# Reordering VectorE's work at the head of the feed-forward stages, and the last two weight loads of each

## The chip, the cores and the metric

The kernel runs on one core of a Trainium2 chip. The metric is device time in microseconds (us) for one execution. The kernel before the change took 2425.06 us (median of 3 runs, 2421.0 to 2426.04). The engines are named as the profile names them: PE is TensorE's matmul, PEld its weight load, DVE VectorE, ACT ScalarE, POOL GpSimd, SP SyncE, which here only issues the loads of the weights.

## What is computed

Two transformer layers work on 256 tokens of width 1024. Each layer has a feed-forward stage, a mixing stage (attention and a convolution) and a second feed-forward stage. After them comes a third, different block, which the change does not touch. All of it is in 32-bit floating point.

```
for l in range(2):
    x = x + 0.5 * swiglu(rms_norm(x, ffn1_norm[l]), gate[l], up[l], down[l])    # F = 2816
    ... attention and convolution on rms_norm(x, mix_norm[l]) ...
    x = x + 0.5 * swiglu(rms_norm(x, ffn2_norm[l]), gate2[l], up2[l], down2[l])
    x = rms_norm(x, post_norm[l])
swiglu(x) = (silu(x @ w_gate) * (x @ w_up)) @ w_down
ada = silu(c) @ w_ada + b      # 48 column tiles; used only by the later block
```

## The kernel before

**Panels.** Weights come from memory in panels of 128 x 1024 numbers (512 KB). SP loads them, in one fixed order, into a ring of 7 slots (`ring`); each load has a wait of its own, for the work that frees its slot, and SP passes its waits in order. A feed-forward stage takes 66 weight panels: for each of its 22 tiles of hidden width a gate panel, an up panel and a down panel. The numbers of its panels are 0 gate, 1 up, 2 gate, 3 up, 4 down, then in each round of a loop with 10 rounds 5, 6 (gate, up), 7 (down), 8, 9 (gate, up), 10 (down), and at the end 65 (down).

**Two halves of a panel.** A product is made of three matmuls on operands that are split into a high and a low part. ACT writes the high part of a panel into one of three slots of `wsplit` (`high`, L1372) as soon as the panel has landed and the panel three before it has been used; DVE writes the low part (`low`, L1998) after that. PE waits for the low part (`low_ready`). A gate or up panel is 24 matmuls of L716, a down panel 12 of L756.

**The hidden activations.** When the up panel of a tile is through, ACT computes the silu (L1467) and DVE multiplies and splits (`gated`, three instructions, L2072 to L2076, which end in `act_ready`). The down panel of the tile waits for that.

**The ada shares.** Of the 48 panels of `w_ada`, 12 are put into each of the four feed-forward stages and worked off by DVE beside the matmuls: one panel is a share, 16 instructions (`ada_products`, L2046 x2 and L2050 x14) that add up in `ada_acc`; PE then adds over partitions (`ada_sum`, L769). Share 0 is loaded ahead of panel 4; share 11 is loaded at the end, its products (`ada_last`) are computed in the stage that follows, and `ada_out` (L2063) puts the 24 sums of a stage into `ada`. In PE's order `ada_sum` of share 0 stands between panel 4 and panel 5, and waits for the products.

**The order.** Every engine's order is that of the code, written out by hand. DVE's at the head of a stage is: low part of panel 3, `gated(0)`, low part of panel 4, half of share 0, low part of panel 5, the rest of share 0, and the loop. In layer 1's first feed-forward stage the products of share 11 of the stage before stand in pieces among the preparations (`spare` in `row_factors`, where DVE waits for ACT) and around panel 3. `normed` (L2033, two instructions) scales the rows of the residual; it stands at the end of the first feed-forward stage of each layer. At the end of a stage SP issues the load of panel 65 (waiting for the low part of panel 59), then that of share 11 (waiting for the products of share 10); the first load of the next stage waits for the low part of panel 65.

In what follows the four feed-forward stages are called F1 (it begins at 16 us), F2 (365), F3 (569) and F4 (911).

## Time and profile before

| | |
|---|---|
| time, median of 3 | 2425.06 us |
| profiled execution: time, span | 2425.06 us, 2423.4 us |
| mean granted TensorE clock | 0.969 of full |
| PE busy | 2285.3 us (94%) |
| DVE busy | 1700.5 us (70%) |
| ACT busy | 1108.0 us (46%) |
| chain that ended last | PE 37%, DVE 12%, issue 2%, ACT 2% |
| weight panels | 539 loads of 512 KB, 4.2 us to landing (median) |

The span is cut in the profile into stretches, and the busy time of an engine is the sum of its instructions there. A busy engine is not the bound wherever it is busy; the argument goes by what each engine waits for at a given place. The four feed-forward stages take 194 to 201 us each.

### The profile page before, as it was taken

How to read it: one execution, taken by the hardware profiler on the slowest of the kernel's cores; microseconds unless marked ns; L12 is line 12 of the kernel's file. 1: busy time of each engine (PE TensorE's matmuls, PEld its weight loads, DVE VectorE, ACT ScalarE, POOL GpSimd, SP SyncE). 2: the span in 40 equal slices, each digit the busy share in tenths (PEclk: the TensorE clock that was granted, in tenths of full speed). 3: DMA queues.
4: the chain of work that ended last, by engine and by line, in shares of the span. 5: the costliest groups of instructions: out<-in, count | busy, mean ns of one | idle time of the engine just before them, and what ended most of it. 6: DMA issues, size and time to landing. Idle time of an engine off the chain costs nothing.

```text
span 2423.4 us, 37828 instructions
## 1 busy us (share of the span) xinstructions
PE 2285.3 (94%) x13712; PEld 1986.6 (82%) x13712; DVE 1700.5 (70%) x3271; ACT 1108.0 (46%) x1769; POOL 87.3 (4%) x140
## 2 busy tenths in 40 slices
PE   7999989998999989996999999999999999999979
PEld 6998769998998769995777778888887888888868
DVE  6877858778877958786445545443547888888884
ACT  4333344335333244334545553333435655556652
POOL 0000000000000000001112101001100000000000
PEclk9999989999999989997999999999999999999989
DMA  7564216554554216553344432221212222222213
GB/s 272 194 227 163 87 58 253 204 203 182 209 212 178 81 58 235 199 208 72 79 76 78 70 97 69 70 70 62 79 44 102 82 83 81 87 87 87 84 47 104
DMA packets 81766, 298.64 MB, mean 123 GB/s; under 512 B 10132, under 2 KB 10644, under 8 KB 80916
## 3 DMA queue, kind: packets, MB, share of 16 engines
q1 hardware_dynamic: 77904, 284.72, 33.6%
q0 software_dynamic: 2048, 4.20, 3.2%
q10 hardware_dynamic: 1736, 8.67, 1.0%
q8 instruction: 49, 0.80, 0.1%
q14 instruction: 29, 0.24, 0.0%
HBM read 296.51 MB, written 1.05 MB: 123 GB/s over the span
## 4 chain that ended last, share of the span: by engine, by line
PE 37%; DVE 12%; issue 2%; ACT 2%; DVEq 0%; ACTq 0%
PE ps L716 28%; PE ps L1308 2%; DVE work L2709 2%; DVE work L2698 2%; DVE wsplit L1998 2%; PE ps L1166 1%; PE ps L1048 1%; PE ps L1062 1%; PE ps L1038 1%; DVE work L2748 1%; DVE work L2679 1%; DVE work L2677 1%; PE ps L1018 1%; PE ps L1286 1%; DVE work L2682 0%
## 5 line engine op out<-in xcount | busy, mean ns | idle before, releaser
L716 PE MATMUL ps<-hsplit,wsplit 128*128 128x256 f32 (+1 forms) x8328 | 1382.6, 324 | 32.8 <-DVE work L2719 17.7
L716 PEld LDWEIGHTS ps<-hsplit,wsplit 128*128 128x128 f32 x8328 | 1204.1, 192 | 163.4 <-issue 33.4
L1372 ACT ACTIVATE wsplit<-ring 128x1024 fp32r<-128x1024 f32 x465 | 491.1, 1057 | 593.5 <-PE ps L716 458.3
L1998 DVE TENSOR_TENSOR wsplit<-ring,wsplit 128x1024 fp32r<-128x1024 f32 x465 | 571.8, 1231 | 264.6 <-ACT wsplit L1372 262.2
L756 PE MATMUL ps<-wsplit,fsplit 128*128 128x512 f32 x1056 | 256.3, 391 | 0.0
L756 PEld LDWEIGHTS ps<-wsplit,fsplit 128*128 128x128 f32 x1056 | 192.7, 188 | 36.3
L2050 DVE SCALAR_TENSOR_TENSOR work<-ring,cs,work 128x128 f32<-128x128 f32 x672 | 206.1, 348 | 8.8
L1467 ACT ACTIVATE work<-ps 128x256 f32<-128x256 f32 x88 | 33.8, 384 | 159.4 <-PE ps L716 159.4
L2162 DVE SCALAR_TENSOR_TENSOR work<-work,vec 128x256 f32<-128x256 f32 x240 | 100.9, 481 | 1.7
L716 PEld LDWEIGHTS ps<-wsplit,hsplit 128*128 128x128 f32 x768 | 95.5, 197 | 4.5 <-issue 3.0
L716 PE MATMUL ps<-wsplit,hsplit 128*128 128x256 f32 x768 | 97.1, 289 | 1.1 <-DVE wsplit L1998 1.1
L2072 DVE TENSOR_TENSOR work<-ps,work 128x256 f32<-128x256 f32 x88 | 37.3, 424 | 81.2 <-ACT work L1467 81.0
L819 PE MATMUL ps<-work,ring 128*128 128x256 f32 x416 | 91.0, 380 | 0.0
L819 PEld LDWEIGHTS ps<-work,ring 128*128 128x128 f32 x416 | 79.1, 191 | 10.6
L2806 POOL DMA_DIRECT2D work<-rpb x64 | 39.4, 624 | 1273.5 <-DVE xT L2033 1130.4
L1715 ACT ACTIVATE work<-ps 128x512 f32<-128x512 f32 (+1 forms) x64 | 31.4, 491 | 115.5 <-PE ps L1048 114.6
L2410 DVE TENSOR_REDUCE work<-ps 128x2 f32<-128x1024 f32 (+1 forms) x32 | 30.7, 958 | 56.7 <-PE ps L1038 56.2
L1308 PE MATMUL ps<-work 128*128 128x128 f32 x512 | 64.6, 282 | 0.0
L1308 PEld LDWEIGHTS ps<-work 128*128 128x128 f32 x512 | 63.3, 199 | 1.2
L1486 ACT ACTIVATE work<-work 128x512 f32<-128x512 f32 (+2 forms) x42 | 28.9, 687 | 67.7 <-DVE work L2145 50.2
L742 PE MATMUL ps<-cst,work 128*128 128x128 f32 x112 | 22.8, 377 | 34.4 <-DVE work L2016 33.8
L2748 DVE COPY_PREDICATED work<-cst,ps 128x256 f32<-128x256 int32 x112 | 50.2, 448 | 3.9
(331 smaller groups left out, 2305.2 us busy)
## 6 DMA issues: line engine op xcount, KB each, us to landing
ring<-panels SPq DMA_DIRECT2D x539, 512.0 KB, 4.2
work<-latent_weights ACTq DMA_DIRECT2D x2, 2304.0 KB, 13.1
work<-rpb POOLq DMA_DIRECT2D x64, 64.0 KB, 7.1
cst<-constants ACTq DMA_DIRECT2D x1, 1408.0 KB
work<-x SPq DMA_DIRECT2D x1, 1024.0 KB, 5.6
work<-post_rows ACTq DMA_DIRECT2D x2, 512.0 KB, 5.7
cT<-ctx ACTq DMA_DIRECT2D x1, 1024.0 KB, 9.3
out<-xT SPq DMA_DIRECT2D x1, 1024.0 KB, 3.9
```

Of the source, the lines that this page charges most:

```text
L716: ins = mm(out_, w(a), x(b), start=start and n == 0, stop=stop and n == 2, **kw)
L756: ins = mm(ps[:, 2 * t + half, :], lhs(a, t), w[:, b, half * 512:(half + 1) * 512], start=first and a == 0 and b == 0, stop=last and a == 1)
L819: last = mm(ps[:, bank, half * T:(half + 1) * T], w[:, k, :], hf[:, k, :], start=k == 0, stop=k == KD - 1)
L1308: last = mm(ps[:, 4 + r % 2, e * T + s * 128:e * T + (s + 1) * 128], k_, q_, start=True, stop=True)
L1372: af(wsplit[:, split_slot(name, n), 0, :], ring[:, p % slots, :], ACT.Copy).then_inc(high_ready, 1)
L1998: tt(parts[:, 1, :], ring[:, p % slots, :], parts[:, 0, :].bitcast(fp32), ALU.subtract)\
L2050: ins = stt(ada_acc[:, v, :], w[:, k, :], factor, ada_acc[:, v, :], ALU.mult, ALU.add)
L2162: ins = stt(acc[:, c, :], u_pad[:, c, j:j + T], w, acc[:, c, :], ALU.mult, ALU.add)
L2698: ins = tt(c_aq[:, lev, :].rearrange("p (n a g) -> p n a g", n=nb, a=2), own, border, ALU.subtract)
L2709: ins = tt(c_ak[:, lev, :].rearrange("p (n a g) -> p n a g", n=nb, a=2), border, own, ALU.subtract)
L2748: ins = nc.vector.copy_predicated(diag, m.unsqueeze(1).to_broadcast([128, 2, 128]), got)
L2806: pool.dma_start(dst.rearrange("p (a w) -> p a w", a=4), src).then_inc(a_bias_loaded, 16)
```

## The change

DVE, at the head of every feed-forward stage: the low part of panel 4 is no longer computed ahead of the products of share 0, nor that of panel 5 in their middle. All 16 products come first, then the loop begins, and its rounds begin with the low parts of the two panels with which they ended before. PE's order is changed in F3 alone, where `ada_sum` of the stage before moves from between panels 2 and 3 to behind panel 3. In the preparations of F3 the products of share 11 no longer fill DVE's waits: the first 8 stand behind the low part of panel 2, the last 8 behind that of panel 3, and `ada_out` ahead of `gated(0)`. `normed` moves from the end of F1 and F3 to their head. SP issues the load of share 11 ahead of that of panel 65.

```diff
--- before.py
+++ after.py
@@ -673,8 +673,8 @@
                     with sp.Fori(0, FT // 2 - 2) as i:
                         for p in (14, 15, 16, 13, 17, 18, 19):
                             again(p, i)
+                    again(len(s.order) - 2)
                     again(len(s.order) - 1)
-                    again(len(s.order) - 2)
                 elif s.panels % s.slots:
                     for p in range(s.slots, s.panels):
                         again(p)
@@ -784,10 +784,9 @@
                                (rows_done, l * 12 + 8 * f + 4) if last else None, i, ready=(act_ready, ready))
 
                 gate_up(0, 0, wait=lambda k: pe.wait_ge(h_ready, h_at(n) + (k + 1)))
-                project(name, l, 2, ps[:, 5, 0:T])
+                gate_up(2, 1)
                 if l > 0 and f == 0:
                     ada_sum(l - 1, 1, ADA_PER_FFN - 1)
-                project(name, l, 3, ps[:, 5, T:2 * T])
                 down(4, 0, fb + 1, first=True)
                 pe.wait_ge(ada_ready, 2 * l + f)
                 ada_sum(l, f, 0)
@@ -2001,23 +2000,19 @@
             def halves(a, b):
                 return a[:, b // 2, (b % 2) * 512:(b % 2 + 1) * 512]
 
-            def row_factors(q, sq0, per, sets, src, firsts=(), spare=None):
+            def row_factors(q, sq0, per, sets, src, firsts=()):
 
                 for t in range(2):
                     dve.wait_ge(sq_ready, sq0 + per * (t + 1))
                     tt(n_ms[:, t, 0:sets], n_ss[:, t, 0:sets, 0], n_ss[:, t, 0:sets, 1], ALU.add).then_inc(row_stage, 1)
                     if t == 0 and firsts:
                         low(*firsts[0])
-                if spare is not None:
-                    spare(range(0, 2))
                 dve.wait_ge(rstd_ready, 3 * q + 1)
                 for half in range(2):
                     c = slice(half * 512, (half + 1) * 512)
                     ts(xs[:, 0, c], src[:, 0, c], n_rr[:, 0:1], None, ALU.mult).then_inc(row_stage, 1)
                 for first in firsts[1:]:
                     low(*first)
-                if spare is not None:
-                    spare(range(2, 4))
 
             def turned(q, gain, banks, name, l):
 
@@ -2076,20 +2071,16 @@
                     tt(fsplit[:, par, 1, :], ff_sil[:, par, :], fsplit[:, par, 0, :].bitcast(fp32), ALU.subtract)\
                         .then_inc(act_ready, 1)
 
-                if l > 0 and f == 0:
-                    ada_last(l - 1, 1, range(4, 6))
                 low(name, l, 3)
                 if l > 0 and f == 0:
-                    ada_last(l - 1, 1, range(6, KD))
+                    ada_last(l - 1, 1, range(4, KD))
+                    ada_out(l - 1, 1)
                 gated(0, fb + 1)
-                low(name, l, 4)
-                if l > 0 and f == 0:
-                    ada_out(l - 1, 1)
-                ada_products(name, l, f, 4, 0, 0, range(0, 4))
-                low(name, l, 5)
-                ada_products(name, l, f, 4, 0, 0, range(4, KD))
+                ada_products(name, l, f, 4, 0)
                 V.restart()
                 with dve.Fori(0, FT // 2 - 1) as i:
+                    low(name, l, 4, i)
+                    low(name, l, 5, i)
                     gated(1, i * 2 + fb + 2)
                     low(name, l, 6, i)
                     ada_products(name, l, f, 6, 1, i, range(0, 2))
@@ -2099,13 +2090,11 @@
                     gated(0, i * 2 + fb + 3)
                     low(name, l, 9, i)
                     ada_products(name, l, f, 6, 1, i, range(5, KD))
-                    low(name, l, 10, i)
-                    low(name, l, 11, i)
                     V.restart()
+                low(name, l, 3 * FT - 2)
+                low(name, l, 3 * FT - 1)
                 gated(1, fb + FT)
                 V.restart()
-                if f == 0:
-                    normed(l)
                 if f == 1:
                     dve.wait_ge(rows_loaded, l * 32 + 48)
                 dve.wait_ge(x_normed, 2 * (l + 1))
@@ -2313,6 +2302,9 @@
                     dve.wait_ge(ada_sig, 1)
                     V.did(tt(cs[:, 1, :], cs[:, 0, :], vec2[:, W_C:W_C + 16], ALU.mult))
                     V.restart()
+                else:
+                    ada_last(l - 1, 1, range(0, 4))
+                normed(l)
                 ffn("ffn1", l, 0)
                 V.restart()
                 row_factors(l * 3 + 1, 16 * l + 4, 2, 1, xN)
@@ -2323,8 +2315,7 @@
                 ffn("ffn2", l, 1)
                 V.restart()
                 row_factors(l * 3 + 3, 16 * l + 12, 4, 2, xg,
-                            (("ffn1", l + 1, 0), ("ffn1", l + 1, 1)) if l + 1 < LAYERS else (),
-                            (lambda tiles: ada_last(l, 1, tiles)) if l + 1 < LAYERS else None)
+                            (("ffn1", l + 1, 0), ("ffn1", l + 1, 1)) if l + 1 < LAYERS else ())
                 if l + 1 < LAYERS:
                     dve.wait_ge(const_loaded, l * 16 + 112)
             def modulation(j):
```

DVE at the head of F1, as its program has it before: the low parts (L1998) of panels 3, 4 and 5 stand around `gated(0)` and the two halves of share 0.

```order
L1998 TENSOR_TENSOR wsplit<-ring,wsplit 128x1024
L2072 TENSOR_TENSOR work<-ps,work 128x256
L2074 CAST fsplit<-work 128x256
L2076 TENSOR_TENSOR fsplit<-work,fsplit 128x256
L1998 TENSOR_TENSOR wsplit<-ring,wsplit 128x1024
L2046 TENSOR_SCALAR work<-ring,cs 128x128 x2
L2050 SCALAR_TENSOR_TENSOR work<-ring,cs,work 128x128 x6
L1998 TENSOR_TENSOR wsplit<-ring,wsplit 128x1024
L2050 SCALAR_TENSOR_TENSOR work<-ring,cs,work 128x128 x8
```

DVE at the same place now (L1997 is the low part, L2028 is `normed`, L2041 and L2045 the products):

```order
L2028 TENSOR_SCALAR xT<-work 128x1024 x2
L1997 TENSOR_TENSOR wsplit<-ring,wsplit 128x1024
L2067 TENSOR_TENSOR work<-ps,work 128x256
L2069 CAST fsplit<-work 128x256
L2071 TENSOR_TENSOR fsplit<-work,fsplit 128x256
L2041 TENSOR_SCALAR work<-ring,cs 128x128 x2
L2045 SCALAR_TENSOR_TENSOR work<-ring,cs,work 128x128 x14
L211 ISA
L2081 UNCONDITIONAL_BRANCH
L2081 ISA
L1997 TENSOR_TENSOR wsplit<-ring,wsplit 128x1024
```

The low parts of panels 4 and 5 moved behind all 16 products and into the loop's beginning; `normed` came in ahead of the low part of panel 3.

DVE in the head of F3 before, from behind the low part of panel 2 on: products of share 11 around the low part of panel 3, then `gated(0)`. L2063 is `ada_out`.

```order
L2050 SCALAR_TENSOR_TENSOR work<-ring,cs,work 128x128 x4
L1998 TENSOR_TENSOR wsplit<-ring,wsplit 128x1024
L2050 SCALAR_TENSOR_TENSOR work<-ring,cs,work 128x128 x4
L2072 TENSOR_TENSOR work<-ps,work 128x256
L2074 CAST fsplit<-work 128x256
L2076 TENSOR_TENSOR fsplit<-work,fsplit 128x256
L1998 TENSOR_TENSOR wsplit<-ring,wsplit 128x1024
L2063 TENSOR_TENSOR ada<-ps,vec 128x24
L2046 TENSOR_SCALAR work<-ring,cs 128x128 x2
L2050 SCALAR_TENSOR_TENSOR work<-ring,cs,work 128x128 x6
L1998 TENSOR_TENSOR wsplit<-ring,wsplit 128x1024
L2050 SCALAR_TENSOR_TENSOR work<-ring,cs,work 128x128 x8
```

The same place now, from the low part of panel 3 on (L2058 is `ada_out`, the ISA row resets DVE's step count):

```order
L1997 TENSOR_TENSOR wsplit<-ring,wsplit 128x1024
L2045 SCALAR_TENSOR_TENSOR work<-ring,cs,work 128x128 x8
L2058 TENSOR_TENSOR ada<-ps,vec 128x24
L2067 TENSOR_TENSOR work<-ps,work 128x256
L2069 CAST fsplit<-work 128x256
L2071 TENSOR_TENSOR fsplit<-work,fsplit 128x256
L2041 TENSOR_SCALAR work<-ring,cs 128x128 x2
L2045 SCALAR_TENSOR_TENSOR work<-ring,cs,work 128x128 x14
L211 ISA
L2081 UNCONDITIONAL_BRANCH
L2081 ISA
L1997 TENSOR_TENSOR wsplit<-ring,wsplit 128x1024
```

`ada_out`, which waits for PE, now stands ahead of `gated(0)` and of all of share 0, and the low part of panel 4 behind them. PE's matching sum stands 24 matmuls later, behind panel 3.

SP at the end of F1, with what each load waits for (the first load behind the branch is panel 65):

```order
L673 REGISTER_ALU
L673 COMPARE_AND_BRANCH
L643 DMA ring<-panels 128x1024 [waits low_ready]
L643 DMA ring<-panels 128x1024 [waits ada_acc_ready]
L643 DMA ring<-panels 128x1024 [waits low_ready] x6
L643 DMA ring<-panels 128x1024 [waits ada_acc_ready]
```

and now:

```order
L673 REGISTER_ALU
L673 COMPARE_AND_BRANCH
L643 DMA ring<-panels 128x1024 [waits ada_acc_ready]
L643 DMA ring<-panels 128x1024 [waits low_ready] x7
L643 DMA ring<-panels 128x1024 [waits ada_acc_ready]
```

The load of panel 65 is now queued behind the wait for share 10's products (`ada_acc_ready`) and the load of share 11.

## Rows read from the trace of the kernel before

**Rows 1.** Timeline, PE in F2's loop: start, us, engine, line, operation, count, idle before.
```profile
395.89 2.91 PE L756 MATMUL ps<-wsplit,fsplit 128*128 128x512 f32 x12
399.00 5.28 PE L716 MATMUL ps<-hsplit,wsplit 128*128 128x256 f32 x42
```

**Rows 2.** Timeline, the head of F2 on DVE and PE.
```profile
373.80 1.22 DVE L1998 TENSOR_TENSOR wsplit<-ring,wsplit 128x1024 fp32r<-128x1024 f32 x1
377.81 2.91 PE L756 MATMUL ps<-wsplit,fsplit 128*128 128x512 f32 x12
378.41 2.56 DVE L2050 SCALAR_TENSOR_TENSOR work<-ring,cs,work 128x128 f32<-128x128 f32 x8
381.01 0.42 DVE L2072 TENSOR_TENSOR work<-ps,work 128x256 f32<-128x256 f32 x1
381.55 6.00 PE L716 MATMUL ps<-hsplit,wsplit 128*128 128x256 f32 x48
```

**Rows 3.** Timeline, DVE: a whole share's 16 products without a break.
```profile
1122.93 0.48 DVE L2046 TENSOR_SCALAR work<-ring,cs 128x128 f32<-128x128 f32 x2
1123.44 4.51 DVE L2050 SCALAR_TENSOR_TENSOR work<-ring,cs,work 128x128 f32<-128x128 f32 x14
```

**Rows 4.** Timeline, the head of F1 on DVE and PE.
```profile
23.78 0.42 DVE L2072 TENSOR_TENSOR work<-ps,work 128x256 f32<-128x256 f32 x1 [0.92 <-ACT work L1467]
24.57 0.43 DVE L2076 TENSOR_TENSOR fsplit<-work,fsplit 128x256 fp32r<-128x256 f32 x1
28.92 2.91 PE L756 MATMUL ps<-wsplit,fsplit 128*128 128x512 f32 x12
36.23 0.98 PE L769 MATMUL ps<-ones,work 128*128 128x1 f32 x4 [4.41 <-DVE work L2050]
37.08 8.59 PE L716 MATMUL ps<-hsplit,wsplit 128*128 128x256 f32 x48
```

**Rows 5.** Timeline, the head of F3 on DVE and PE.
```profile
571.80 1.23 DVE L1998 TENSOR_TENSOR wsplit<-ring,wsplit 128x1024 fp32r<-128x1024 f32 x1
582.67 2.91 PE L756 MATMUL ps<-wsplit,fsplit 128*128 128x512 f32 x12
587.51 6.00 PE L716 MATMUL ps<-hsplit,wsplit 128*128 128x256 f32 x48
```

**Rows 6.** Timeline, PE's first transposes behind F1 and F3; then a window: us, busy, clock, DMA.
```profile
220.07 3.38 PE L742 MATMUL ps<-cst,work 128*128 128x128 f32 x16 [2.52 <-DVE work L2016]
...
767.91 2.09 PE L742 MATMUL ps<-cst,work 128*128 128x128 f32 x16 [2.52 <-DVE work L2016]
...
565.70:575.70 10.00, 9.78 (x58) 0.68 0.01 3
```

**Rows 7.** Loads of the ring (L643): share 11 in F1; then two issued together at 758.6.
```profile
L643 SPq DMA_DIRECT2D ring<-panels x1: 338/338/338, 207.3 to 207.3; - x1
...
DMA to landing us min/median/max: 3.3/3.8/4.4
```

**Rows 8.** Timeline, the end of F1 on ACT, DVE and PE.
```profile
208.41 1.06 ACT L1372 ACTIVATE wsplit<-ring 128x1024 fp32r<-128x1024 f32 x1 [1.81 <-PE ps L716]
211.65 0.42 DVE L2072 TENSOR_TENSOR work<-ps,work 128x256 f32<-128x256 f32 x1 [0.92 <-ACT work L1467]
212.77 1.41 DVE L2033 TENSOR_SCALAR xT<-work 128x1024 f32<-128x1024 f32 x2
214.14 2.97 PE L756 MATMUL ps<-wsplit,fsplit 128*128 128x512 f32 x12
```

**Rows 9.** Timeline, ACT behind the end of F2 and of F4.
```profile
557.30 1.06 ACT L1372 ACTIVATE wsplit<-ring 128x1024 fp32r<-128x1024 f32 x1 [0.24 <-DMA ring<-panels]
558.27 0.63 ACT L1391 ACTIVATE work<-xT 128x512 f32<-128x512 f32 x1
...
1102.04 1.06 ACT L1372 ACTIVATE wsplit<-ring 128x1024 fp32r<-128x1024 f32 x1 [1.18 <-DMA ring<-panels]
1104.34 0.63 ACT L1391 ACTIVATE work<-xT 128x512 f32<-128x512 f32 x1 [1.24 <-DVE xT L2117]
```

## The prediction

> **What bounds the kernel now.** I read the shares of busy time first, then PE's timeline through a feed-forward stage, then the timelines of all engines at the four heads (F1 to F4) and ends. In the loops of the stages PE is the bound: matmuls stand back to back with no idle time, and a down panel with the ada sum behind it takes 3.11 us from its start to that of the next gate panel [rows 1]. So what DVE does there costs nothing, while what PE waits for at a head or an end is added to the time, since nothing behind it is ahead of PE. At the four heads PE waits before the sum of share 0: 4.41 us in F1 [rows 4], and in F2 the next gate panel starts 3.74 us after the down panel where 3.11 is normal [rows 2]. At the ends PE runs into panel 65 at once; normed lies in DVE's idle time [rows 8].
>
> **Head of F2 and F4.** Before, DVE makes the low part of panel 4 right behind gated(0), from 373.80, and PE takes that panel at 377.81, when panel 3 is through: 2.8 us of reserve. Now the 16 products come first. A whole share takes 0.51 + 4.51 = 5.02 us [rows 3]. The loop's entry costs 0.04 us: before, it stood between the last product (378.41 + 2.56 = 380.97) and 381.01 [rows 2]. The low part starts at 373.80 + 5.02 + 0.04 = 378.86, ends 1.22 later at 380.08, and PE starts at about 380.2, which is 2.4 us late. The wait for the share's products goes, so the gate panel follows 3.11 us later, at 383.3, where it was 381.55. Net 1.75 us. The low part of panel 5 follows in DVE at once (381.3) and is in time. Twice (F2, F4): +3.5 us. The bounds of each are 1.75 and, if the clock falls in the idle 2.4 us, about 2.7 more (below).
>
> **Head of F1.** gated(0) ends at 25.0 [rows 4], the products at 29.95, the low part of panel 4 at 31.2; PE starts panel 4 at 31.3 instead of 28.92. But there it then waited 4.41 us for the products, and its clock fell: the 48 matmuls of panels 5 and 6 took 8.59 us from 37.08 [rows 4], where 6.0 is normal [rows 2]. Now they start at 31.3 + 3.11 = 34.4 and end at 40.4 instead of 45.67, so -5.3 us. If the clock falls in the new wait too (2.4 us), only -2.6. Here normed costs nothing: it takes 1.41 us [rows 8] in a time in which DVE waits for ACT's high part of panel 3; if that cover were gone, it would delay a low part whose panel PE reaches two panels later.
>
> **Head of F3.** Here a chain forms. Low part of panel 2 at 571.80 [rows 5]; then 8 products of share 11 (2.5), normed (1.4), the low part of panel 3, ready at about 578, in time for PE, which begins panel 3 some 3 us ahead of 582.67. Eight more products end at 580.4. Then ada_out waits for PE's sum, which now comes behind panel 3: panel 3 ends at about 582.4 (before, with that sum ahead of it, PE went on to panel 4 at 582.67 [rows 5]), the sum takes 0.5 (half of the 0.98 at half clock in [rows 4]), so 582.9. Only then DVE does ada_out (0.2), gated(0) (24.57 + 0.43 - 23.78 = 1.22 [rows 4], 1.13 to the next start), the share (5.02), the entry (0.04) and the low part (1.22), while PE has nothing: 582.9 + 0.2 + 1.13 + 5.02 + 0.04 + 1.22 + 0.1 = 590.6, which is 7.9 us late. The old wait at the sum (587.51 - 582.67 - 3.11 = 1.73 us) goes, so 6.2 us. With PE idle for 7.7 us the clock will fall. [...] I take 3.1, so +9.3 us. Bounds 7.5 (the smallest cost in a row, 3.38 - 2.09 = 1.3 us for the transposes [rows 6]) to 9.4. What the pieces in row_factors cost before, 0.2 us ahead of DVE's scaling, is hidden by ACT's scaling of the other rows, so taking them out gives nothing; the loads that wait for share 11 come 3 us later, which PE's new wait covers.
>
> **The ends.** SP passes its waits in order. Before, panel 65 was loaded in the round before; now it stands behind share 11, which can be loaded only when share 10 is through, at 207.3 in F1 [rows 7]. Its issue follows 0.43 us later. Of two loads issued together the first lands after 3.3 us, the second 4.4 us after its issue [rows 7]. So panel 65 lands at 207.34 + 0.43 + 4.4 = 212.1. ACT began its high part at 208.41 [rows 8], now 3.7 us later: high 212.2 to 213.2, low to 214.4, and gated(1), which is queued behind it in DVE, to 215.5 (it began at 211.65). PE starts panel 65 at 215.6 instead of 214.14, +1.5 us, in F1 and F3 each: +3.0. Behind F2 and F4 more hangs on it. The next stage's first load waits for the low part of panel 65, so it too is 3.7 us late, and ACT makes the high parts of the first panels before the squares that all the rest waits for. Behind F2 the second high part ran from 557.30 to 558.36 and the squares began at 558.27 [rows 9]; now they begin 3.8 us late. I give back 0.4, because the eight squares then find their data ready: +3.4. Behind F4 only one panel stands ahead of the squares: 1102.04 + 3.7 + 1.06 = 1106.8 against 1104.34 [rows 9], 2.5 less 0.3: +2.2. The ends together: 8.6 us. If panel 65 landed 3.3 us after its issue like the first of a pair, each would cost 1.1 less, so the lower bound is 4.2; the upper, with no time given back and a landing a little later, is 10. The two moved low parts in the loop start in the same order, with the loop's branch ahead instead of behind: 0.
>
> [...]
>
> **The sum.** -5.3 + 3.5 + 9.3 + 8.6 = +16.1 us. The profiled execution took 2425.06 us around its span of 2423.4 and is itself the median of the three, so the sum is added to it: 2441.2, say 2441 us.
>
> **Rivals.** (1) *The clock falls in the short waits too.* After the same 2.52 us of idle time the same 16 transposes took 3.38 us once and 2.09 once [rows 6]: the clock had fallen behind F1 and not behind F3, so the rows speak for neither. In F1, F2 and F4 each fall costs some 2.7 us: 2441 + 8 = 2449 us. [...] (2) *The ends are hidden.* If panel 65 lands in time after all (SP's queue was free, and ACT has 3 us at its head), only the heads remain: 2425 + 7.5 = 2432.5 us. Against it: the issue at 207.3 and the shortest landing of 3.3 us [rows 7] are behind 208.41 together. (3) *Faster.* The wait at share 0's sum goes in all four heads: 5.3 + 0.6 + 1.7 + 0.6 = 8.2 us. If the low part of panel 4 were still in time, that would be a gain. It decides at 377.8 in F2: the share would have to take under 2.6 us where it takes 5.02. With the ends hidden that is 2417 us, with them 2425. Against it stands DVE's own row of 14 products in 4.51 us. (4) *No difference:* the delays of the heads and ends fall into later waits for loads or for ACT, and the gain of F1 cancels the rest; 2425 us. The loops without idle time speak against it, since a stage is a fixed number of matmuls.
>
> **How the numbers follow.** Forecast 0.60; (1) 0.17; (2) 0.13; (4) 0.06; (3) 0.04. The forecast's own range by the bounds of its terms is 2435 to 2443 (-5.3 + 3.5 + 7.5 + 4.2 = 9.9 at the low end, 17.6 at the high end without a fall of the clock); with (1) and most of (2) the range is 2432 to 2449 us. What a measurement can tell from no change is about 0.2% or 4.9 us; the cases above give slower 0.92, the same 0.05, faster 0.03.
>
> **What would show it.** In the profile after: PE's idle time before panel 4 released by DVE's low part, about 2.3 us in F1, F2 and F4 and near 8 in F3; no wait at the sum of share 0; F1's panels 5 and 6 in about 6 us; the load of panel 65 issued right behind that of share 11, its high part released by a DMA; PE idle some 1.5 us before the last down panel of each stage; in the preparations of F3 squares that start behind the second high part. It would be wrong if PE's first wait in a head stayed at the sum, if the idle time in F3 were under 5 us, or if the ends showed no idle time.

## The result, and the profile after

The changed kernel takes 2449.17 us (median of four runs, 2445.18 to 2450.23), the kernel before on the same chip 2425.55 us (2421.0 to 2428.47): ratio 1.0099, 95% interval 1.0081 to 1.0117. It is slower, as forecast, but by 23.6 us where the forecast was 16.1, and lies just above the range. In a second batch it took 2447.05 us against 2427.39 (1.0086, 1.0073 to 1.0100); the two together say +20 to +24 us. The profiled execution of the changed kernel took 2451.94 us and is not one of the four; the rows below are from it (span 2450.3 us).

The page after, its busy line and the group of PE's down panels (count | busy us, mean ns | idle time before, releaser):

```profile
PE 2300.0 (94%) x13712; PEld 1997.2 (82%) x13712; DVE 1708.0 (70%) x3271; ACT 1107.3 (45%) x1769; POOL 86.0 (4%) x140
...
L756 PE MATMUL ps<-wsplit,fsplit 128*128 128x512 f32 x1056 | 265.6, 402 | 19.7 <-DVE wsplit L1997 14.2
```

The count is that of before. The idle time is new (it was 0.0), 14.2 us of it before the low part of a weight panel; and the matmuls themselves became slower, 402 ns instead of 391 on the mean, and 265.6 us of busy time instead of 256.3. Of these 9.3 us the forecast's sum has only the part in F3.

PE's waits of the changed kernel, 10 to 1160 us (total, times, longest):

```profile
PE ps L756 <- DVE wsplit L1997: 14.6, 6, 7.6
...
PE ps L769 <- DVE work L2045: 6.2, 1, 6.2
PE ps L756 <- DVE fsplit L2071: 5.5, 4, 1.6
```

The first row holds the four heads (2.21, 2.18, 7.61 and 2.18 us), the last the four ends (1.13 to 1.65). The one wait left at an ada sum is behind F4, where the kernel before waits too; the four at share 0 are gone.

PE's timeline at the heads of F1, F2 and F3 after (start, us, line, count, idle before), to be laid beside [rows 2, 4, 5]:

```profile
32.39 3.01 PE L756 MATMUL ps<-wsplit,fsplit 128*128 128x512 f32 x12 [2.21 <-DVE wsplit L1997]
35.24 0.50 PE L769 MATMUL ps<-ones,work 128*128 128x1 f32 x4
35.60 6.00 PE L716 MATMUL ps<-hsplit,wsplit 128*128 128x256 f32 x48
...
379.87 4.60 PE L756 MATMUL ps<-wsplit,fsplit 128*128 128x512 f32 x12 [2.18 <-DVE wsplit L1997]
...
588.61 0.50 PE L769 MATMUL ps<-ones,work 128*128 128x1 f32 x4
596.71 5.43 PE L756 MATMUL ps<-wsplit,fsplit 128*128 128x512 f32 x12 [7.61 <-DVE wsplit L1997]
```

The waits are within 0.3 us of the forecast (2.4, 2.4, 7.9). F1's panels 5 and 6 take 6.00 us instead of 8.59, as forecast. But the same 12 matmuls behind the same wait take 3.01 us in F1 and 4.60 in F2 (2.91 in the loops). The granted clock tells them apart. Three windows of the same trace: the panel in F1, the wait in F2, and the panel in F2 (the numbers behind the busy times are the clock, the DMA share and GB/s):

```profile
32.50:35.20 2.70, 2.70 (x12) 2.24 (x13) 2.63 (x5) 1.06 (x1) 0.00 (x0) 1.00 0.89 316
...
377.70:379.80 2.10, 0.00 (x0) 0.00 (x0) 2.02 (x5) 1.33 (x2) 0.00 (x0) 1.00 0.44 129
380.50:383.00 2.50, 2.50 (x8) 1.93 (x7) 2.43 (x5) 0.00 (x0) 0.00 (x0) 0.50 0.91 295
```

In F2 the clock still reads 1.00 through the wait and is at half (0.50) within the panel behind it. Where this text says that the clock fell in or behind a short wait, it means these slow matmuls.

The chain in F3, on DVE:

```profile
584.43 2.56 DVE L2045 SCALAR_TENSOR_TENSOR work<-ring,cs,work 128x128 f32<-128x128 f32 x8
589.14 0.18 DVE L2058 TENSOR_TENSOR ada<-ps,vec 128x24 f32<-128x24 f32 x1 [2.15 <-PE ps L769]
...
590.36 0.48 DVE L2041 TENSOR_SCALAR work<-ring,cs 128x128 f32<-128x128 f32 x2
590.87 4.51 DVE L2045 SCALAR_TENSOR_TENSOR work<-ring,cs,work 128x128 f32<-128x128 f32 x14
595.43 2.36 DVE L1997 TENSOR_TENSOR wsplit<-ring,wsplit 128x1024 fp32r<-128x1024 f32 x2
```

It is the forecast's chain link by link: DVE waits at 589.14 for PE's sum of 588.61, then come gated(0), the whole share, and only about 596.65 is the low part of panel 4 ready (half of the last row).

The ends: the two loads of F1's end as they are issued by SP, then ACT's high part of panel 65 in F1 and the first high parts behind F2, then PE's last down panel in F1, F2 and F3 (views in this order, each with its idle time; beside [rows 7 to 9]):

```profile
L643 SPq DMA_DIRECT2D ring<-panels x2: 338/380/423, 203.3 to 203.7; - x2
...
DMA to landing us min/median/max: 3.2/3.6/4.1
```

```profile
207.75 1.06 ACT L1371 ACTIVATE wsplit<-ring 128x1024 fp32r<-128x1024 f32 x1 [5.22 <-DMA ring<-panels]
...
563.18 1.06 ACT L1371 ACTIVATE wsplit<-ring 128x1024 fp32r<-128x1024 f32 x1 [3.32 <-DMA ring<-panels]
564.43 1.06 ACT L1371 ACTIVATE wsplit<-ring 128x1024 fp32r<-128x1024 f32 x1 [0.19 <-DMA ring<-panels]
565.40 0.61 ACT L1390 ACTIVATE work<-xT 128x512 f32<-128x512 f32 x1
```

```profile
211.34 3.00 PE L756 MATMUL ps<-wsplit,fsplit 128*128 128x512 f32 x12 [1.13 <-DVE fsplit L2071]
...
560.82 4.58 PE L756 MATMUL ps<-wsplit,fsplit 128*128 128x512 f32 x12 [1.55 <-DVE fsplit L2071]
...
778.59 4.58 PE L756 MATMUL ps<-wsplit,fsplit 128*128 128x512 f32 x12 [1.65 <-DVE fsplit L2071]
```

Panel 65, the second of the pair, lands 4.1 us after its issue (4.4 forecast), so ACT waits for a DMA where it waited for PE. Again the waits are as forecast (1.5), and in F2 and F3 the 12 matmuls behind them take 4.58 us (granted clock 0.60 in both, 561.0 to 565.3 and 778.7 to 783.0 us), as at the low clock in the head of F2.

**Where the time went, stage by stage.** Differences of the stages' lengths, from PE's timeline, us. The last column is experiment 5 below: both kernels with PE kept busy in nearly all of its waits; beside it the forecast without its clock terms. The rows are differences of two traces, and the kernel before differs from itself by 0.9 us up to F1's second down panel, 2.7 in mixing stage 1, 1.4 in F3 and 1.7 in mixing stage 2 (experiment 3).

| stage | forecast | after − before | forecast, no clock | both kept busy |
|---|---|---|---|---|
| F1, up to its second down panel | −5.3 | −4.1 | −2.7 | −4.3 |
| F1, its end | +1.5 | +1.3 | +1.5 | +1.6 |
| mixing stage 1 | 0 | +2.5 | 0 | +0.1 |
| F2, head and end | +5.2 | +6.8 | +5.2 | +5.1 |
| F3, head and end | +10.8 | +11.7 | +7.7 | +7.6 |
| mixing stage 2 | 0 | +1.5 | 0 | +1.4 |
| F4, head and end | +3.9 | +5.1 | +3.9 | +3.5 |
| behind F4 | 0 | +2.1 | 0 | −3.2 |
| sum of the traces | +16.1 | +26.9 | +15.6 | +11.8 |
| medians | | +23.6 | | +14.3 |

**Behind F4.** This part of the kernel has no edit, and its +2.1 us is not a draw. From the transposes behind F4 to the end the kernel before takes 1311.79 and 1311.63 us in two traces, the changed kernel 1313.86 and 1313.89. All traces divide the same way: the five with the two loads swapped and PE's other waits not filled take 1313.8 to 1314.4 us, the seven with the loads in the old order and no fillers 1310.6 to 1311.8. In the traces of before and after 1.0 us is lost in the first 40 us and 3.0 more from 353 to 379 us in; some 1.5 us of it are back by 460 us, and 2.1 are left at the end. First the kernel before, then the changed one:

```profile
1474.92 11.77 PE L716 MATMUL ps<-wsplit,hsplit 128*128 128x256 f32 x96
```

```profile
1501.65 13.89 PE L716 MATMUL ps<-wsplit,hsplit 128*128 128x256 f32 x96
```

The granted clock is 1.00 all through the first row; in the second it is 0.50 until about 1506. So the swap of the loads goes with a cost of some 2 us in a block that it doesn't touch, through the clock. Why the slow stretch there grows with it is open; with fillers the order is lost (1313.85 for the kernel before, 1310.69 for the changed one, 1308.31 for the changed one with its heads alone filled).

### The profile page after: what moved, and what is told of

Same layout as the page of the kernel before. It is cut to its first block, busy times and chain, and to the rows that moved or that the text cites. A ratio compares the mean times of both kernels' runs of the same rounds, so it can differ in the third digit from the quotient of the medians.

```text
span 2450.3 us, 37828 instructions
## 1 busy us (share of the span) xinstructions
PE 2300.0 (94%) x13712; PEld 1997.2 (82%) x13712; DVE 1708.0 (70%) x3271; ACT 1107.3 (45%) x1769; POOL 86.0 (4%) x140
## 4 chain that ended last, share of the span: by engine, by line
PE 37%; DVE 12%; issue 2%; ACT 2%; DVEq 0%; ACTq 0%
PE ps L716 28%; PE ps L1307 2%; DVE work L2700 2%; DVE work L2689 2%; DVE wsplit L1997 2%; PE ps L1165 1%; PE ps L1047 1%; PE ps L1061 1%; PE ps L1037 1%; DVE work L2739 1%; DVE work L2670 1%; DVE work L2668 1%; PE ps L1017 1%; PE ps L1285 1%; DVE work L2673 0%
## 5 line engine op out<-in xcount | busy, mean ns | idle before, releaser
L1997 DVE TENSOR_TENSOR wsplit<-ring,wsplit 128x1024 fp32r<-128x1024 f32 x465 | 574.8, 1238 | 270.9 <-ACT wsplit L1371 258.3
L756 PE MATMUL ps<-wsplit,fsplit 128*128 128x512 f32 x1056 | 265.6, 402 | 19.7 <-DVE wsplit L1997 14.2
L756 PEld LDWEIGHTS ps<-wsplit,fsplit 128*128 128x128 f32 x1056 | 198.7, 194 | 59.2 <-DVE wsplit L1997 14.9
L2045 DVE SCALAR_TENSOR_TENSOR work<-ring,cs,work 128x128 f32<-128x128 f32 x672 | 206.0, 348 | 9.0
```

Source lines behind the costliest of these rows:

```text
L756: ins = mm(ps[:, 2 * t + half, :], lhs(a, t), w[:, b, half * 512:(half + 1) * 512], start=first and a == 0 and b == 0, stop=last and a == 1)
L1997: tt(parts[:, 1, :], ring[:, p % slots, :], parts[:, 0, :].bitcast(fp32), ALU.subtract)\
L2045: ins = stt(ada_acc[:, v, :], w[:, k, :], factor, ada_acc[:, v, :], ALU.mult, ALU.add)
```

## The experiments

Theory: the waits are as summed, and what is missing is PE's clock, which falls in the short waits too. Rivals: the clock falls by chance, or the missing time is something else. All ratios are to the kernel before on the same chip; in the five batches its medians were 2425.55 to 2427.39 us.

**1. The swap of the loads, put back and alone.**

```
 after_loads_back (changed kernel)     swap_only (kernel before)
-                    again(len(s.order) - 2)      |  -  again(len(s.order) - 1)
                     again(len(s.order) - 1)      |     again(len(s.order) - 2)
+                    again(len(s.order) - 2)      |  +  again(len(s.order) - 1)
```

> The changed kernel with one edit: panel 65 is loaded ahead of share 11 again. Theory A: the heads alone are left, 2449 - 8.6 = 2440.5 us. Theory B: 2449 less 10 to 13, so 2436 to 2439 us. In the profile no idle time before the last down panels; in F2 and F4 the head should still wait 2.2 us. Rival C: 2449 us.

> The kernel before with one edit: SP issues the load of share 11 ahead of that of panel 65. Theory A (waits at the ends, as the prediction summed them): about 1.5 us behind F1 and F3, 3.4 behind F2, 2.2 behind F4, so +8.6 us, 2434 us. Theory B (the idle time before panel 65 also lets PE's clock fall, as the profile after showed in F2 and F3, where the last down panel took 4.6 us instead of 3.0): the same waits and 1.5 to 3 us more behind F1 and F3, so +10 to +13 us, 2436 to 2438. Rival C (the ends are hidden in the next stage): 0, 2425 us.

Measured: put back 2438.2 us (ratio 1.0044, 1.0031 to 1.0058), so the swap costs 9 to 11 us on top of the heads, and theory B's range holds. Alone 2443.35 us (1.0066, 1.0052 to 1.0080), +16.7, more than either theory said. Its trace has waits of 1.38, 1.28, 1.19 and 1.23 us before the last down panels, 5.1 us in all; from the second down panel to the transposes its four stages are 1.5, 3.2, 1.4 and 1.6 us longer, 7.7 in all. (The 8.6 that one expectation below calls the sum of the four waits is the forecast's number for the ends.) Another 2.3 us stand behind F4; the rest is in stages without an edit.

**2. The heads alone, and F3's chain alone.** heads_only moves the low parts of panels 4 and 5 behind the share in DVE's program of the kernel before, f3_only moves share 11, ada_out and PE's sum as the change does and leaves panel 4's low part ahead of share 0.

```
 heads_only:                                   f3_only:
-                low(name, l, 4)               |  -  ada_last(l - 1, 1, range(4, 6))
                 (ada_out)                     |     low(name, l, 3)
-                ada_products(..., range(0, 4))|  +  ada_last(l - 1, 1, range(4, KD))
-                low(name, l, 5)               |  +  ada_out(l - 1, 1)
-                ada_products(..., range(4,KD))|     gated(0, fb + 1)
+                ada_products(name, l, f, 4, 0)|     low(name, l, 4)
```

> The kernel before with one edit: all 16 products of share 0 stand ahead of the low part of panel 4, and the loop begins with the low parts of its two panels; share 11's products, PE's order, normed and the loads stay. Theory A (waits alone): F1 -5.2, F2 and F4 +1.75 each, F3 +2.0 (low part of panel 4 at 585.0 instead of 578.4, PE 3.7 later at panel 4, less 1.7 for the wait at the sum), sum +0.3 us, 2426 us. Theory B (the clock falls in waits of 2.2 us and more): 1.6 us more in each of F2, F3 and F4, and F1's gain given back by up to 3 us in the mixing stage behind it, where the narrow matmuls then run at half clock: +5 to +8 us, 2430 to 2433 us.

> The kernel before with the edits to F3 alone: share 11's products behind the low parts of panels 2 and 3, ada_out ahead of gated(0), PE's sum behind panel 3; the low part of panel 4 stays ahead of share 0. Theory A: the low part of panel 4 ends at 582.9 + 0.2 + 1.13 + 1.22 = 585.5, PE is 3.0 us late there; the share then ends at 591.7, and the next gate panel starts at 592.2 instead of 587.51: +4.7 us, 2430 us. Theory B: 1.5 us more for the clock, which falls in the first or the second of these waits: +6.2 us, 2432 us. Rival: ada_out's wait is covered by DVE's other work: under +1 us.

Measured: heads_only 2431.95 us (1.0026, 1.0017 to 1.0035), within B's range and 6 above A's; f3_only 2430.64 (1.0016, 1.0007 to 1.0025), A's number. PE's timeline shows why the first follows B; the heads of F1 and F3 in heads_only, of F3 in f3_only, and of F2 in the changed kernel with its loads back:

```profile
33.44 4.38 PE L756 MATMUL ps<-wsplit,fsplit 128*128 128x512 f32 x12 [3.72 <-DVE wsplit L1998]
...
588.28 4.35 PE L756 MATMUL ps<-wsplit,fsplit 128*128 128x512 f32 x12 [3.52 <-DVE wsplit L1998]
```

```profile
582.63 4.61 PE L756 MATMUL ps<-wsplit,fsplit 128*128 128x512 f32 x12 [2.53 <-DVE wsplit L1997]
```

```profile
377.89 4.60 PE L756 MATMUL ps<-wsplit,fsplit 128*128 128x512 f32 x12 [2.19 <-DVE wsplit L1997]
```

Two things came out otherwise than both theories had it. In heads_only the gain of F1 is 1.9 and 1.0 us against the two traces of before, not 5.2: share 0's load lands later there (DVE waits 1.43 us for it), PE waits 3.72 us before panel 4, and the clock falls in F1 too (4.38 us). And in f3_only the clock did fall behind the wait of 2.53 us (4.61 us for the panel), as B said; F3 is 5.7 and 4.3 us longer than in the two traces of before, so A's number in the median does not show that the clock stayed up.

**3. Both kernels once more, without an edit.**

> The changed kernel once more, without an edit, for a second trace of it. Theory A (the clock's falls hang on how long PE waits and on what stands around the wait): they stand at the same places as in the first trace: in the wait of 2.2 us at the heads of F2 and F4 (the down panel takes 4.6 us instead of 2.9), in the waits before the last down panel of F2 and F3 (4.6 us), not in those of F1 and F4 (3.0 us), not in the head of F1, and in mixing stage 1 the 20 ones-matmuls take 4.4 us instead of 2.4. Theory B (they are chance): the waits are the same within 0.2 us, but at half of these places or more the clock is the other one. The time is 2449 us by both; by B single runs lie 4 us or more apart.

> The kernel before once more, without an edit, for a second trace of it, above all of mixing stage 1, where PE's clock gave back 4 us of what the head of F1 had gained. Theory A: the 32 matmuls, the 20 ones-matmuls and the first 12 of the diagonal block take 3.65, 2.37 and 5.81 us again, and the first wait of F1 is 4.4 us. Theory B: in this trace one of the three is 1 us or more longer, without any edit. About 2426 us.

Measured: after_again 2447.05 us, before_again 2429.85 us (one run). Both theories are right, each at its own places. The heads repeat within 0.2 us: 4.59, 5.30 and 4.61 us in F2, F3 and F4 behind waits of 2.18, 7.61 and 2.19, and F1 3.01 us again. The end of F3 does not, and mixing stage 1 doesn't even between two traces of the kernel before. First PE's end of F3 in after_again; then the narrow matmuls of mixing stage 1 in the trace of before, and in before_again:

```profile
779.34 3.00 PE L756 MATMUL ps<-wsplit,fsplit 128*128 128x512 f32 x12 [1.22 <-DVE fsplit L2071]
```

```profile
272.42 2.37 PE L847 MATMUL ps<-ones,work 128*128 128x1 f32 x20
274.65 5.81 PE L855 MATMUL ps<-work 128*128 128x480 f32 x12
```

```profile
272.79 4.20 PE L847 MATMUL ps<-ones,work 128*128 128x1 f32 x20
276.86 5.60 PE L855 MATMUL ps<-work 128*128 128x480 f32 x12
```

So mixing stage 1 is 142.7 us long in one trace and 145.4 in the other, with the same program. The +2.5 of the table's third line is no larger than that and shows no loss of F1's gain, as I had first read it. The head of F1 differs too: in before_again PE waits 1.23 us before panel 4 and 3.42 at the sum, and panels 5 and 6 take 7.49 us where they took 8.59.

**4. PE kept busy in the four new waits.** In the changed kernel PE does matmuls that nobody reads, as long as the wait (the code is abridged).

```
+                for _ in range(9 if (l, f) != (1, 0) else 30):
+                    mm(ps[:, 7, :] ..., hsplit[:, 0, 0, 0:128], hsplit[:, 0, 0:2, :], start=True, stop=True)
                 down(4, 0, fb + 1, first=True)
```

> The changed kernel with matmuls that PE does in its new waits at the four heads: ahead of the first down panel 9 matmuls of 512 columns into a bank that nobody reads (some 2.2 us), 30 in F3 (7.3 us). The waits for DVE stay as long as they were. Theory A (the fall of the clock in these waits is a cost of its own, +1.6 us in F2 and F4, 2.5 in F3): the three down panels take 2.9 to 3.0 us, the idle time ahead of them is under 0.5 us, and the time is some 5.7 us under that of the changed kernel, 2443 us; F1, where the clock did not fall, is unchanged. Rival B (the panel was slow because its operands or the bank arrive late, not because of the clock): it takes 4.6 us still, and the time stays at 2449 us. Rival C: the idle time is what costs, and the clock falls elsewhere instead: 2449 us with 2.9 us at the three panels.

Measured: 2437.32 us (1.0050, 1.0037 to 1.0064), 9.7 below after_again in the same batch. The head of F2:

```profile
376.02 2.23 PE L795 MATMUL ps<-hsplit 128*128 128x512 f32 x9
378.37 3.02 PE L756 MATMUL ps<-wsplit,fsplit 128*128 128x512 f32 x12
```

The panel takes 3.02 us instead of 4.60 (granted clock 1.00 instead of 0.60) with the same operands at the same distance behind DVE: rival B, that its data came late, falls. From the first to the second down panel the heads of F2, F3 and F4 are 1.6, 2.3 and 1.6 us shorter, 5.5 in all, which is the price of the clock there. The other 4 us of the 9.7 I don't claim for the fillers: the two traces differ by 5.6 us behind F4 (1308.3 and 1313.9) and by 2.2 in mixing stage 1 (2.37 us for its 20 matmuls in this trace and 4.41 in after_again), where nothing was edited.

**5. PE kept busy in nearly all waits, in both kernels and in the swap.** Besides the heads: 5 such matmuls before the last down panel (not in the kernel before, which doesn't wait there), 9, 11 and 23 before the transposes of the stages, 13 and 5 before the sum of share 0 where it is still waited for.

```
+                keep(9)
                 pe.wait_ge(x_ready, l * 16 + 4)
                 turn(l * 3 + 1, MIX_BANKS)
...
+                if f == 0:
+                    keep(13 if l == 0 else 5, 7)
                 pe.wait_ge(ada_ready, 2 * l + f)
                 ada_sum(l, f, 0)
```

> The kernel before with matmuls of 512 columns that nobody reads in PE's waits: 13 ahead of the sum of share 0 in F1 (3.2 us of the wait of 3.4 to 4.4), 5 in F3, 9 ahead of the transposes behind F1 and F3, 11 behind the mixing stages, 23 behind F2 and F4. No wait is shortened. Theory A (waits cost twice, once as idle time and once by the slow clock behind them): F1's panels 5 and 6 take 6.0 us instead of 8.6 (-2.6), the transposes 2.1 us instead of up to 3.6 (four stages, -1 each), the first panels of F2 to F4 start at full clock (-1 to -3 each): 10 us in all, 2417 us. Theory B (the clock falls by chance, the gain is lost again in mixing stage 1, or the fillers end behind the waits): 2424 to 2429 us.

> The changed kernel with such matmuls in its waits too: 9 ahead of the first down panel (30 in F3), 5 ahead of the last down panel of each stage, and those ahead of the transposes. Against the kernel before with its waits filled it shows what the change costs at full clock throughout. Theory A (the waits are as I summed them, and the rest of the +21 to +24 us is clock): F1 -2.7, F2 and F4 +1.75 each, F3 +6.2, the ends +8.6, so +15.6 us over that kernel, within 2: 2433 us if that is 2417. Rival B (the difference of the two kernels is not in the clock): +20 us or more over it.

> The kernel before with the two last loads of a feed-forward stage swapped, alone, and all its waits filled, also 5 matmuls ahead of the last down panel. Without fillers this swap cost 16.7 us where its four waits in the trace sum to 8.6. Theory A (the other 8 us are the clock, in the waits ahead of the last down panel and by chance in mixing stage 1): +8.6 us over the kernel before with its waits filled, within 2: 2426 us if that is 2417. Rival B (the late load of panel 65 costs something else than these waits, in the later block for one): +13 us or more over it, and the trace names a wait that stands in no feed-forward stage.

Measured: before_kept 2424.68 us (0.9993, 0.9984 to 1.0002), after_kept 2439.02 (1.0056, 1.0042 to 1.0069), swap_kept 2429.57 (1.0019, 1.0008 to 1.0029). The change costs 14.3 us between the filled kernels, where my waits sum to 15.6: theory A's difference holds. In the table above it holds in F2, F3, F4 and at F1's end, but not in F1's head (−4.3 where the waits say −2.7). There one wait of before_kept was not filled, and the clock fell in it:

```profile
30.41 4.62 PE L756 MATMUL ps<-wsplit,fsplit 128*128 128x512 f32 x12 [2.74 <-DVE wsplit L2008]
```

So before_kept isn't at full clock throughout: in its trace 1.6 us of the −4.3 are that fall. The swap costs 4.9 us between the filled kernels; from the second down panel on its four stages are 7.5 us longer in the traces.

Theory A was wrong on the kernel before itself: filling its waits gave 1.9 us, not 10. PE at the head of F3 in before_kept shows where part of that gain goes:

```profile
579.12 2.91 PE L756 MATMUL ps<-wsplit,fsplit 128*128 128x512 f32 x12
581.87 1.29 PE L776 MATMUL ps<-hsplit 128*128 128x512 f32 x5
584.36 0.58 PE L769 MATMUL ps<-ones,work 128*128 128x1 f32 x4 [1.20 <-DVE work L2060]
```

The stage's first panels run faster, so PE starts panel 4 15.5 us after the transposes instead of 17.0, but DVE's share 0 isn't ready any earlier: the next gate panel starts 5.68 us after panel 4 where it was 4.84 [rows 5]. This head, which DVE bounds, hands a faster PE a longer wait.

**6. The swap again, and only its own waits filled.**

> The swap of the two last loads alone once more, without an edit, for a second trace. Its median was 16.7 us over the kernel before, while the four waits in its trace sum to 8 us and the changed kernel is only 9 to 11 us over itself with the loads put back. Theory A (the swap's own waits are 8 us; the rest is the clock, which falls in some executions in the waits ahead of the last down panel and in mixing stage 1): the waits are 1.2 to 1.6 us again; the median lies within 2 us of 2443; in this trace at least one of the four last down panels takes 4.6 us instead of 3.0, or mixing stage 1 is slow as in the first trace. Theory B (16.7 was a draw of that batch): the median is 2437 us or less.

> The swap alone with 5 matmuls of 512 columns that nobody reads ahead of the last down panel of each stage and no other filler; they keep PE busy in the wait that the swap makes (1.2 to 1.6 us) and leave its length. Theory A (part of the 16.7 us is the clock in or behind these four waits): 4 us or more below the swap alone of the same batch. Rival B (the clock is lost elsewhere by chance): within 2 us of it.

Measured: 2439.86 us (1.0049, 1.0035 to 1.0063) and 2440.18 us (1.0058, 1.0044 to 1.0072). The swap's first median was a high draw, its second is +12.7; in its trace the last down panel of F2 takes 4.56 us behind a wait of 1.67, and mixing stage 1 is slow (4.22 us for its 20 narrow matmuls). Filling only these four waits changes nothing (rival B). So of the swap's 12.7 to 16.7 us some 8 are the longer ends of the stages (7.7 and 8.1 in the two traces), and 2.0 to 2.6 stand behind F4 in all three traces of the swap without the full set of fillers. The slow panel in F2 costs little: that end is 3.6 us longer with it and 3.2 without. The remaining 3 to 7 us are not settled; mixing stage 1, which varies by itself, is 147.0 and 144.1 us in the two traces.

**7. Two ways to a faster kernel.** sum_later moves PE's sum one panel later in every round, and in DVE the whole share 0 behind the low parts of panels 4 and 5 (in the loop five tiles of a share behind the low part of 7); f1_split divides share 0 in F1 alone; split_kept is f1_split with the fillers of 5.

```
 sum_later (PE)                                       f1_split (DVE)
-                ada_sum(l, f, 0)              |       gated(0, fb + 1)
                 with pe.Fori(0, FT // 2 - 1)..|  +    if first: ada_products(..., range(0, 3))
-                    gate_up(5, 0, i)          |       low(name, l, 4)
+                    project(name, l, 5, ...)  |       ada_out(l - 1, 1)          (not in F1)
+                    ada_sum(l, f, 0, i)       |  +    ada_products(..., range(3, KD))  (in F1)
+                    project(name, l, 6, ...)  |       low(name, l, 5)
```

> The kernel before with PE's sum of a share one panel later instead of DVE's order changed around it: in each round of the loop the sum stands between the two gate panels 5 and 6, so that share 0 may come 2.9 us later; DVE makes the low parts of panels 4 and 5 and then the whole share 0, and in the loop the low parts of 6 and 7 ahead of five tiles of the share. Theory A (what the change ran into was the order of PE: the first share had a deadline that DVE's order alone cannot meet): PE's waits at the sum of share 0 go in all four heads (4.4, 0.4, 1.5 and 0.4 us) with the slow clock behind that of F1 (2.6 us), 9.3 us in all, of which mixing stage 1 may give back up to 4: 2417 to 2421 us. Rival B (DVE is now late with the low part of panel 6 in the heads, or of 7 or 8 in every round, because the share's products move behind them): idle time before gate panels in the loops, 0.3 us or more a round, 40 rounds, 2426 us or more.

> The kernel before with only the order of DVE in F1's head changed: 3 tiles of share 0 ahead of the low part of panel 4, the other 5 behind it, the low part of panel 5 last; no fillers. It tells how much of the 5.2 us of the candidate comes from this. Theory A: PE's waits in F1 (4.4 us at the sum) become about 1.4 to 2 us before panel 5, the clock does not fall there, so the 48 matmuls take 6 us: -3 to -5 us, 2422 to 2424 us. Rival B (the low part of panel 4 is late, and mixing stage 1 takes the rest back): 2425 us or more.

> A candidate to beat both: the kernel before with its waits filled, and in F1 alone DVE's share 0 divided otherwise: 3 tiles ahead of the low part of panel 4, which PE reaches 2 us after it is made, the other 5 right behind it, the low part of panel 5 last. The whole wait at the sum in F1 (4.4 us) becomes one of 1.4 us before panel 5. Theory A: 3 us under the kernel before with its waits filled, 2414 us if that is 2417. Rival B (the share's load lands too late, at 25.6 to 27 us, so that the low part of panel 4 waits with it): within 1 us of that kernel or above it.

Measured: sum_later 2427.91 us (1.0005, 0.9996 to 1.0014), no gain; f1_split 2422.18 (0.9980, 0.9971 to 0.9989); split_kept 2421.35 (0.9979, 0.9970 to 0.9988). First PE in F1 of sum_later, then of f1_split:

```profile
33.58 3.14 PE L716 MATMUL ps<-hsplit,wsplit 128*128 128x256 f32 x24 [0.81 <-DVE wsplit L1999]
38.62 0.60 PE L769 MATMUL ps<-ones,work 128*128 128x1 f32 x4 [1.90 <-DVE work L2051]
39.82 3.14 PE L716 MATMUL ps<-hsplit,wsplit 128*128 128x256 f32 x24 [0.60 <-DVE wsplit L1999]
```

```profile
29.99 3.03 PE L756 MATMUL ps<-wsplit,fsplit 128*128 128x512 f32 x12 [0.72 <-DVE wsplit L1998]
33.21 0.58 PE L769 MATMUL ps<-ones,work 128*128 128x1 f32 x4 [0.19 <-DVE work L2050]
35.26 6.02 PE L716 MATMUL ps<-hsplit,wsplit 128*128 128x256 f32 x48 [1.48 <-DVE wsplit L1998]
```

In sum_later the one wait has become three, since DVE's work in the head is the same and PE reaches each piece at its own time; from the first to the second down panel F1 takes 13.0 us (16.6 and 14.2 in the two traces of before), and mixing stage 1, without an edit, is 147.4 us in this trace. In f1_split the wait of 4.41 us [rows 4] becomes 0.72, 0.19 and 1.48, and panels 5 and 6 take 6.02 us. F1 up to its second down panel is 4.4 and 3.6 us shorter than in the two traces of before. The fillers add nothing that can be told: 5.2 us under the kernel before against 5.0, each in its own batch. f1_split beats the kernel before by 5.0 us and the changed one by some 26.

Why it gains is read from DVE. The first row is the low part of panel 4 in the kernel before and the second that of panel 5; then the three tiles and the low part of panel 4 in f1_split:

```profile
27.31 1.23 DVE L1998 TENSOR_TENSOR wsplit<-ring,wsplit 128x1024 fp32r<-128x1024 f32 x1 [2.32 <-ACT wsplit L1372]
...
32.38 1.23 DVE L1998 TENSOR_TENSOR wsplit<-ring,wsplit 128x1024 fp32r<-128x1024 f32 x1 [1.50 <-ACT wsplit L1372]
```

```profile
25.61 1.26 DVE L2050 SCALAR_TENSOR_TENSOR work<-ring,cs,work 128x128 f32<-128x128 f32 x4
28.71 1.23 DVE L1998 TENSOR_TENSOR wsplit<-ring,wsplit 128x1024 fp32r<-128x1024 f32 x1 [1.84 <-ACT wsplit L1372]
```

Before, DVE stood idle for 2.32 us ahead of the low part of panel 4 and for 1.50 ahead of that of panel 5, each time for ACT's high part, with share 0's products queued behind. These 3.8 us stand in the chain for whose end PE then waited 4.41 us. The high part of panel 5 in turn had waited 4.01 us for its load. f1_split puts three tiles into the first of these waits and moves the second behind the share. The panel-4 reserve of 2 us that its expectation names isn't there in F1: the low part is ready 0.4 us ahead of PE in one trace of before, and 1.2 us late in the other. The expectation of 3 us under before_kept for split_kept was met (3.3).

## Why the prediction was too low

**Right: the direction, the mechanism and the sizes of the waits.** Panel 4's low part 2.2 us late in F1, F2 and F4 (2.4 forecast), F3's chain through ada_out with 7.6 (7.9), no wait left at share 0, panel 65 landing behind a DMA, 1.1 to 1.65 us idle before the last down panels (1.5), the squares behind the second high part in F2. Without the clock the forecast's sum was 15.6 us, and between the kernels kept busy it is 14.3, though one of the two has a fall of the clock left in F1. Normed costs nothing in the traces, as the forecast said; its move was not run alone.

**Wrong: the term for the clock in the short waits, which was set to nothing.** In "Head of F2 and F4" the sum took 1.75 us each and left a fall of the clock to the bounds. It fell in all eight of these heads that four traces show (the changed kernel twice, with its loads back, heads_only), at 1.6 us each, so that each head costs 3.4 us: +3.3 in the two traces of the changed kernel. That is the step that failed, and it repeats.

**Wrong: nothing was taken for the block behind F4.** It costs 2.1 us in both traces of the changed kernel, and goes with the swap of the loads.

The other terms were near. The ends were forecast at 8.6 us and take 9.8 and 8.0 in the two traces (1.3, 3.4, 3.4, 1.7 and 1.3, 3.8, 1.4, 1.5). The clock, which "The ends" doesn't mention, costs there 1.6 us where it falls in F3 (one trace of two). In F2 it falls in both, but that end is 3.2 to 3.5 us longer in the five traces with swapped loads in which it doesn't fall, and 3.4 to 3.8 in the three in which it does, so it adds 0.6 us at most. No run shows the 3.1 us that the sum takes for F3's clock, an estimate of the author's: in the traces that cost is 2.3 to 2.6 us (the panel takes 5.30 to 5.47 us, and 3.01 in after_filled or 2.91 in the loops), at a granted clock of 0.51 (597 to 602 us, after). F3's head costs 8.3 and 8.0 us of 9.3. In F1 the gain was 4.1 us of 5.3 in the first trace, because the 96 matmuls ahead of panel 4 took 14.27 us where they took 13.14 before; in the second they took 13.21, PE started panel 4 at 31.37 (31.3 forecast), and the gain was 5.1.

By the traces, then, of the 7.5 us between 16.1 and 23.6, 3.3 are the clock in the heads of F2 and F4 and 2.1 the block behind F4. The rest is not settled: it is as large as the draws of the mixing stages and of the ends. Rival 1 named the right mechanism and came within 0.2 us of the measured median, in part by luck: it charged 2.7 us in each of F1, F2 and F4, where it was 1.6 in two of them and nothing in F1, and it had nothing behind F4. My argument against it, one fall and one non-fall in [rows 6], was evidence from two draws of a stretch behind ends that differ; a bound of 2.7 us that holds half the time would have been 1.3 in the sum. And the chances don't add as stated: the cases give slower 0.90, the same 0.06 and faster 0.04.

How the clock goes with the length of the wait: behind the long wait of F3 (7.61 us) the panel took 5.43, 5.30 and 5.47 us (after, after_again, after_loads_back), where it takes 2.91 in the loops. For the short ones nothing that goes by the length alone fits the traces: behind 2.18 to 2.21 us the panel took 4.6 us in F2 and F4 and 3.01 us in F1, in the same three traces.

The other rivals: the ends were not hidden (in F1 the loads of the pair landed 3.2 and 4.1 us after their issue, panel 65 as the second). The cases of a gain and of no difference fell at the first wait.

## What to carry to other kernels

An idle gap on TensorE can have two prices, its length and slow work behind it: in F2 2.18 us idle and then 4.60 us for a panel of 3.01, in F1 2.21 us and no slow panel. Take the second into the sum where similar gaps show it, at half weight if they show it half the time. Before moving work of a helper engine, list each piece with the time at which its input is there and the time at which the bound engine reaches it: the kernel improved when part of a late piece was put into a wait of the helper (f1_split, ratio 0.9980), and got worse when the whole of it went ahead of a piece that was needed (heads_only, 1.0026). And take two traces of the kernel before: a stage without an edit can differ by 2.7 us between them (mixing stage 1), while another repeats within 0.2 us (the block behind F4), and there a difference of 2 us counts.

## What the runs showed of the hardware

- The length of a wait alone doesn't tell whether the clock falls. Behind 2.2 us it fell in F2 and F4 in eight cases of eight (0.56 to 0.60 over the panel behind the wait) and in F1 in none of three (1.00); in F1 it did fall behind 2.74 (before_kept, 0.59) and 3.72 us (heads_only, 0.65), in F3 behind 2.53 (f3_only, 0.59). Before the last down panels it had fallen behind 1.55, 1.63, 1.65 and 1.67 us (0.60 to 0.62), but not behind 1.90 (F3 in after_filled), nor in the fifteen cases from 1.11 to 1.43 us.
- The same binary gives different clocks in the same place: 2.37 and 4.20 us for the 20 narrow matmuls of mixing stage 1 in two traces of before, at a granted clock of 1.00 and 0.52 (4.41 us and 0.50 in both of the changed kernel). From the transposes behind F4 to the end the time is steadier: two traces of one kernel agree within 0.4 us there, three pairs of three (before, after, the swap).
- A reordering can cost time far behind the place where it acts: the swap of two loads goes with 2.0 to 2.6 us more behind F4, in five traces of five (1313.8 to 1314.4 us against the 1311.8 of before; without fillers in the other waits).
- Keeping PE busy in its waits raised the mean granted clock from 0.969 to 0.973 in the kernel before and changed the time by nothing that can be measured (0.9993, 0.9984 to 1.0002): part of what it won came back as a longer wait for DVE in F3 (5.68 us from panel 4 to the next gate panel instead of 4.84).
